# Fetching the second tile of x through ScalarE's DMA queue

## What is computed

```
def rmsnorm(x, g):
    xf = x.astype(jnp.float32)
    y = xf * lax.rsqrt(jnp.mean(xf * xf, axis=-1, keepdims=True) + EPS)
    return (y * g.astype(jnp.float32)).astype(x.dtype)

def first_block(x, norm_mix_g, w_in, ...):
        h = rmsnorm(x, norm_mix_g[l])
        proj = h @ w_in[l]
        ... = jnp.split(proj, offsets, axis=-1)
        # mLSTM, short convolution, stick-breaking attention, gates, output and MLP
```

## Time and profile before

| | |
|---|---|
| median of 3 runs | 915.60 us |
| the profiled execution's own time | 915.87 us |
| its span, first to last instruction | 914.2 us |
| TensorE busy | 903.5 us (99%) |
| VectorE busy | 605.8 us (66%) |
| ScalarE busy | 489.0 us (53%) |
| GpSimd busy | 44.3 us (5%) |
| DMA traffic | 163.92 MB, mean 179 GB/s |

### The profile page before, as it was taken

How to read it: one execution, slowest core, us unless ns; L and a number is a source line. 1 busy time by engine, 2 the same in 40 slices (tenths; PEclk the granted TensorE clock), 3 DMA queues, 4 the chain that set the end, 5 groups by cost and what they waited for, 6 DMA issues and landing times. The chain is left out here.

```text
span 914.2 us, 12499 instructions
## 1 busy us (share of the span) xinstructions
PE 903.5 (99%) x5137; PEld 779.1 (85%) x5137; DVE 605.8 (66%) x637; ACT 489.0 (53%) x570; POOL 44.3 (5%) x79
## 2 busy tenths in 40 slices
PE   8999999999999999999999999999999999999997
PEld 7988887789998888888888888889987888888886
DVE  5776766567887445556677755557796677777643
ACT  6434787873435433345555543537777765555441
POOL 1110111110010000000000000001000010000000
PEclk9999999999999999999999999999999999999999
DMA  9676453444255565555565556544842475556641
GB/s 301 221 247 214 138 177 125 160 138 139 92 184 184 186 203 201 194 190 201 167 199 187 185 194 203 201 141 144 277 139 92 132 237 185 184 185 207 207 162 47
DMA packets 99438, 163.92 MB, mean 179 GB/s; under 512 B 4856, under 2 KB 37384, under 8 KB 99253
## 3 DMA queue, kind: packets, MB, share of 16 engines
q1 hardware_dynamic: 99380, 163.11, 54.5%
HBM read 162.04 MB, written 3.16 MB: 181 GB/s over the span
## 5 line engine op out<-in xcount | busy, mean ns | idle before, releaser
L1566 DVE TENSOR_TENSOR wlo<-land,whi 128x2048 fp32r<-128x2048 f32 (+2 forms) x152 | 334.9, 2206 | 164.2 <-ACT whi L1132 163.8
L1132 ACT ACTIVATE whi<-land 128x2048 fp32r<-128x2048 f32 (+1 forms) x152 | 280.3, 1847 | 202.1 <-PE acc L596 145.6
L602 PE MATMUL acc<-xT,whi 128*128 128x256 f32 x336 | 97.2, 289 | 0.0
L606 PE MATMUL acc<-xT,wlo 128*128 128x256 f32 x336 | 95.1, 283 | 0.0
L604 PE MATMUL acc<-xT,whi 128*128 128x256 f32 x336 | 95.0, 283 | 0.0
L594 PE MATMUL acc<-whi,xT 128*128 128x512 f32 (+2 forms) x240 | 91.6, 382 | 0.0
L595 PE MATMUL acc<-wlo,xT 128*128 128x512 f32 (+2 forms) x240 | 90.3, 376 | 0.0
L596 PE MATMUL acc<-whi,xT 128*128 128x512 f32 (+2 forms) x240 | 90.1, 376 | 0.0
L637 PE MATMUL acc<-xT,whi 128*128 128x512 f32 x288 | 69.4, 391 | 0.2 <-DVE gu L2234 0.2
L637 PE MATMUL m<-xT,whi 128*128 128x512 f32 x288 | 68.7, 391 | 0.0
L602 PEld LDWEIGHTS acc<-xT,whi 128*128 128x128 f32 x336 | 64.3, 191 | 2.9 <-issue 2.6
(11 more groups left out here) (410 smaller groups left out, 1515.0 us busy)
## 6 DMA issues: line engine op xcount, KB each, us to landing
land<-in_w_in SPq DMA_DIRECT2D x55, 1024.0 KB, 5.2
land<-in_w_up SPq DMA_DIRECT2D x16, 1024.0 KB, 5.2
land<-in_w_down SPq DMA_DIRECT2D x16, 1024.0 KB, 5.1
land<-in_w_ffn_gate SPq DMA_DIRECT2D x22, 512.0 KB, 4.1
land<-in_w_ffn_up SPq DMA_DIRECT2D x22, 512.0 KB, 5.3
land<-in_w_ffn_down SPq DMA_DIRECT2D x10, 1024.0 KB, 5.0
land<-in_w_in SPq DMA_DIRECT2D x14, 512.0 KB, 4.7
land<-in_w_out SPq DMA_DIRECT2D x6, 1024.0 KB, 5.0
```

The lines of the kernel that those rows point to most:

```text
L602: mm(to, whi[:, s, k, cs], xh[:, k0 + k, :], start=first and c % 2 == 0, stop=False, skip_group_check=True)
L606: last = mm(to, wlo[:, s, k, cs], xh[:, k0 + k, :], start=False, stop=end, skip_group_check=True)
L1132: activate(whi[:, u % PARTS, 0:m, 0:w], land[:, u % LANDS, 0:m, 0:w], ACT.Copy).then_inc(hi_ready, 1)
L1566: v.tensor_tensor(wlo[:, u % PARTS, 0:m, 0:w], land[:, u % LANDS, 0:m, 0:w], whi[:, u % PARTS, 0:m, 0:w].bitcast(F32), ALU.subtract).then_ ...
```

## The change

The second tile of x is no longer issued by SyncE between `lead` and the weights. It is issued by ScalarE, as the first instruction of its list, ahead of the table load and the small activation. Size, destination and semaphore are the same. The two loads of x are then in the queues of two different engines.

```
     @block.sync
     def _(sp):
-        for t in range(TT):
-            sp.dma_start(x_tok[:, t, :], dram["x"][t * P:(t + 1) * P, :]).then_inc(x_in[t], 16)
-            if t == 0:
-                sp.dma_start(lead[:, :], dram["lead"]).then_inc(lead_in, 16)
+        sp.dma_start(x_tok[:, 0, :], dram["x"][0:P, :]).then_inc(x_in[0], 16)
+        sp.dma_start(lead[:, :], dram["lead"]).then_inc(lead_in, 16)
...
+        nc.scalar.dma_start(x_tok[:, 1, :], dram["x"][P:T, :]).then_inc(x_in[1], 16)
         act.wait_ge(heat_set, 1)
         link(activate(root[:, 0:1], ymlT_hi[:, 0, 0:1].bitcast(F32), ACT.Square))
         act.wait_ge(lead_in, 16)
```

## The result

The changed kernel takes 917.75 us in the median of 22 runs (915.86 to 918.09), the kernel before 915.45 us in the median of 22 (915.02 to 916.03). The ratio, which goes by the means, is 1.0019, with a 95% interval of 1.0012 to 1.0025: slower by a fifth of a per cent. The ratio of the medians is 1.0025. The median hides what happens: the runs of the changed kernel lie on **two levels**. Eight are between 915.86 and 916.29, fourteen between 917.46 and 918.09, and none lies between. The kernel before has one level. The lower level is 0.6 us over the kernel before, the upper one 2.4. The forecast was 915.5 with a range of 915.0 to 917.2: the median lies 0.55 us above its top.

What follows compares the result with a forecast made beforehand. TensorE fills the body, and the weight path sets the first product. Weights -0.15 us, ScalarE 0, x path hidden: first product at 9.83, 915.45 against the median, put at 915.5 us; range 915.0 to 917.2.

Steps and rivals of the forecast that it cites:

- Where the path goes: Start: weights issued near 1.7 us, table load near 1.2, transposes at 6.2, no wait for x before tile 1's transposes.
- The sharing: Start: tile 1's packets take turns with tile 0 and `lead`, which land at 6.2 us, 1.35 us late.
- The clock: TensorE's early work: clock still up about 6 us despite the pause, first product possible at 9.65 us, hidden behind weights.
- rival B: Start: x path takes over, clock low for longer; 0.5 to 1.6 us late, 916.1 to 917.2 us; chance 0.34.
- A: The forecast case: weights set the start, 0 to 0.48 us gained, 915.1 to 915.6 us; chance 0.47.
- T0: Start: time when tile 0 and `lead` have landed and TensorE's first transposes begin, taken as 6.2 us.
- The change touches the start alone: Whole kernel: only the start changes; the first product's shift moves the end by nearly as much.
- The weights: Start: SyncE issues later loads 0.48 us earlier; gain at the weights' cast bounded by that, taken as 0.15 us.
- signs of being wrong: Changed timeline: tile 0 landing near 4.6 us, weights over 0.5 us earlier or at all later, or body idle time changed.

Runs made afterwards that it cites:

- e10: Kernel before with one issue less in SyncE's list (two 32 KB weight loads made one), no second queue: 916.03 us median.
- e5: Kernel before, all on SyncE's queue, with `lead` issued behind both tiles of x: 917.22 us median.
- e7: Kernel before, unchanged, run again for a second trace: 915.46 us median.
- e8: Kernel before with eleven warm matmuls instead of seven ahead of the transposes: 915.82 us median.
- e9: Changed kernel with one more issue in SyncE's list (gate weight load cut in two), restoring its old length: 916.48 us median.
- e12: Changed kernel with transposes by banks, eleven warm matmuls ahead, none between tiles, SyncE's list padded: 914.52 us median, ratio 0.9991.
- e14: As e12, but all loads on SyncE's queue in the order tile 0, tile 1, `lead`, weights: 914.63 us median, ratio 0.9993.
- e11: As e12, but with seven warm matmuls ahead instead of eleven: 915.74 us median.
- e2: Changed kernel without the four warm matmuls between the transposes of tile 0 and tile 1: 916.06 us median.
- e6: Changed kernel with ScalarE's issue of tile 1 moved behind its small activation: 918.47 us median.

## Why the prediction was wrong

**Where the path goes: right.** SyncE's weight issue near 1.7 (1.69), the table load near 1.2 (1.22), no cost on ScalarE, the first transposes at 6.2 (6.19), no wait for x between the tiles: all as forecast. The sharing was priced by bytes and stretches, and the price held.

**The clock: the step that failed.** The forecast took the clock to be up near 6 us in spite of the pause, with a chance of 0.47, and rival B took it to be low for longer, with 0.34. Of 22 runs 14 were B's, and 8 the forecast's; in the traces with that pause the clock was up by the end of it in one (5.35 us) and at 9.18 to 10.96 in four. With the 0.6 us of the tail taken off, the lower level (915.3 to 915.7) is about A's 915.1 to 915.6, and the upper one (916.9 to 917.5) lies about the top of B's 916.1 to 917.2. B's own steps are close: a first product at T0 + 3.6 + 1.45 = 11.24, measured 11.40. Part of that is luck: the two parts were 3.47 and 1.74 us, since the clock was low through tile 1's transposes too, until 10.96, which no step had. So the likeliest case was the wrong one, and I had counted them as exclusive. They are two outcomes of one program. Nothing in a trace of before could say with which share; the pause of 1.5 us was written down as the reason for B and then given the smaller chance. A slowdown of over 0.2% had been given 0.09.

**The baseline of B: 0.5 us too late.** B was priced against a first product at 9.98, that of the trace, and added to the median. The trace was of an execution 0.4 us above its median (915.87 against 915.45), and other traces of the same program have 9.47 and, with e10's same start, 9.22. Against the 9.47 the upper level's 11.3 to 11.4 is 1.8 to 1.9 us late, not 1.3 to 1.4, and 1.8 is what e5 shows in its times. I had the sign of it before me: the profiled time stood 0.27 us over the median, and I put nothing on its account.

**The tail: missing.** "The change touches the start alone" was false by 0.6 us. It shortens SyncE's list by an issue, and with that length the tail is 6.65 to 6.67 us instead of 6.04 to 6.06. This term alone lifts the whole result, both levels. 915.45 + 1.8 + 0.6 = 917.85 is the upper level (its 14 runs are at 917.46 to 918.09), and 915.45 + 0.6 = 916.05 the lower (915.86 to 916.29). Without the tail the upper level would be 917.25, and the median at the very edge of the range. So two terms failed together: the clock, which was given the wrong likeliest case, and the tail, which stood at nothing. The body was right: its idle time is 1.94 us in the changed kernel as well.

**The weights: undersized.** I took 0.15 us of gain; the cast came 1.43 us earlier in the trace and 0.4 to 1.7 us earlier, trace against trace. The term was bounded by the issue's 0.48 us, on the ground that the engines are busy anyway. But what changed is the rate from 4.9 to 7.0 us, 254 to 315 GB/s in the four traces of the old order (before, e7, e8, e10) and 387 now. Weights over 0.5 us earlier were among my own signs of being wrong, and in the first pair of traces that sign came. It changed nothing in the result, because the x path was behind it in both levels: at 7.59 + 0.69 = 8.28 the cast was done in e9, and the first product came at 9.52. In e12 it sets the first product.

**The rule on issuing engines.** The Trainium skill says in "DMA: Bandwidth & Descriptors", section "Issuing engines are not separate DMA queues", that issuing from several engines saves only the issuing time. The delay of tile 0 and `lead` by 1.3 us agrees with the interleaving that it describes. The weights' gain does not come out of it: 1.43 us in the first pair of traces and 1.06 between the means of the six and the four, against 0.48 of issue saved. But e5 and e14 have part of that gain on one queue, and the closest pair (8.48 and 8.05) stays within the 0.48. The prediction also calls the sharing "rival B"; it is in the forecast too, which took the same T0 of 6.2. What divides the two is the clock.

## What to carry to other kernels

Before a start is rearranged, ask which of the transfers TensorE waits for *first*, and not which wait is the last one visible: here two transfers of 512 KB, issued together on two queues, landed together near 6 us and the small load behind them 1.3 us later than before; and work that was put in to bridge a wait stands on the path once the wait is gone. A kernel that warms TensorE up on purpose should do so until its data is there; a pause of 1.5 us in that work can leave the outcome to chance, and then a kernel has two times, which a median of three runs may miss. And an edit that changes only the *number* of DMA issues in SyncE's list can lengthen a tail that nothing hides: compare the tail, and the instruction queue's packets in it, before an effect of half a microsecond is put down to the change itself. Last, place the trace among its kernel's runs before a baseline is read from it; here it was 0.4 us above the median.

## What the runs showed of the hardware

- With 206 DMA issues in SyncE's list an 8 KB instruction packet (queue q14) comes 4.62 to 4.64 us behind the start of the last matmul, among the last stores, and the tail is 6.65 to 6.67 us (five traces). With 207 it comes at 1.10 to 1.28, and the tail is 6.04 to 6.06 (nine traces). This holds with and without a second DMA queue in use.
- After a pause of 1.3 to 1.5 us in early work, TensorE's clock was up at 5.35 us in one trace (e9) and at 9.18 (e11), 10.52 (e5), 10.86 (e2) and 10.96 (the changed kernel) in four. With no wait over 0.31 us before the first transposes it was up at 5.28 to 7.46 in nine traces. In e6 it fell at 9.24, in a pause from 7.29 to 9.54, and was up again at 12.65.
- A transfer of 512 KB issued at 0.79 us on ScalarE's queue landed with its twin of SyncE's by 6 us (5.1 and 4.9 us after the issue). Issued at 2.31 us, beside weights, it kept TensorE waiting until 9.54 (e6).
